# Thirty-two experts, 96 places each, packed four to three tiles of 128 rows

## The chip, the cores and the metric

The kernel runs on one core of one Trainium2 chip. The metric is the device time of one execution in microseconds (us), lower is better. All arithmetic is in float32. The core has a matrix engine (PE, with its weight loads shown as PEld), three engines for elementwise work (DVE, ACT, POOL), a queue engine that mostly issues transfers (SP), and 16 DMA engines.

## The reference, cut to what matters

One layer of a decoder over 1024 prompt tokens and 8 sample tokens. Projections, sparse attention, a gated spatial mixer and the first layer norm come first and are not touched by the change. What matters is the last part, a mixture of experts: 4 groups of 8 experts, each token takes the best group and the best two experts in it.

```python
def hierarchical_moe(x, ...):
    lg = (xt @ w_router_group + b_router_group)
    gsel = jnp.argmax(lg, axis=-1)
    ...
    vals, eidx = lax.top_k(le_sel, 2)
    pw = jax.nn.softmax(vals, axis=-1) * pgsel[:, None]
    ...
    for g in range(N_GROUPS):          # 4 groups of 8 experts
        hg = silu(einsum('td,edf->tef', xt, w_expert_gate[g])) * einsum('td,edf->tef', xt, w_expert_up[g])
        out = out + einsum('tef,efd->td', hg * wg[:, :, None], w_expert_down[g])
```

Here d is 1024 and f is 256, so an expert has 2 MB of gate and up weights and 1 MB of down weights. 1032 tokens with two experts each give 2064 (token, expert) pairs, 64.5 for an expert on average. Counted from the reference's inputs, the fullest expert has 82 and none has over 96.

## The kernel before, in words

The program is a row of stages, each its own block of five engine programs joined by a barrier. Two of them matter here.

`merge_and_route` (L1353 to L1677) goes through 9 tiles of 128 tokens. PE multiplies by `w_o` (`project`, L1515), DVE adds and normalizes, PE turns the rows and makes the router's logits (`route`), DVE picks the two experts (`pick`, L1607), PE counts how many earlier tokens chose each expert (`rank`, L1545), and DVE makes of rank and expert the address of the pair in a table in device memory, `list_of` (`place`, L1627). POOL writes the two entries of each token with indirect DMAs (L1487). Before, expert e with rank r has the address 32 r + e, so that column e of a 128 x 32 table holds the first 128 pairs of expert e. SP loads the weights of experts 0 and 1 in this stage (L1461, L1462; `W_AHEAD` is 2).

`experts` (L1680 to L1908) then runs once for ranks 0 to 127. A second pass (L2178) is run only if an expert has more than 128 pairs. For each expert, POOL gathers 128 rows of `h` with an indirect DMA (L1760), whatever the number of real entries; PE turns them in 8 transposes (`turn_rows`, L1796); PE makes gate and up, 128 x 512, over 8 slices of the contraction (`make_hidden`, L1786); ACT and DVE make silu(gate) * up; PE turns that (`turn_hidden`, L1804) and makes the result, 128 x 1024, over 2 slices (`make_result`, L1813); ACT and DVE copy it out; POOL scatters it to `pair_out` (L1768), leaving out the rows of empty entries. The weights stand in `W_BUFS` = 4 buffers. A single semaphore per buffer, `w_in`, stands for both its transfers. Each float32 matmul of the program is two passes, that is two MATMUL and two LDWEIGHTS instructions in the trace.

What sets the order is `staggered`, a written software pipeline: at step i PE runs `turn_hidden(i-2)`, `make_hidden(i-1)`, `turn_rows(i)`, `make_result(i-2)`. A hardware loop covers four experts in its body. POOL goes in program order: gather e, then scatter e - 3, each after its waits. SP goes in program order too: the table's entries, then experts 2 and 3 (behind `rows_in`, so that the first two gathers come first), then expert e as soon as both halves of the result of expert e - 4 are made (L1744, semaphore `down`). `Finish` is the last stage's work: it loads `pair_out`, adds the two halves with PE (L1984, L1994) and makes the second layer norm.

Of the kernel before, what the change touches and what calls it, by code (L numbers as in the profile page):

```python
# [13 lines left out]
I32 = mybir.dt.int32  # L14
U32 = mybir.dt.uint32
ALU = mybir.AluOpType
# [3 lines left out]
P = 128  # L20
D = 1024
# [1325 lines left out]
W_AHEAD = 2  # L1347
SLOTS = TOK * N_EXPERTS
# [4 lines left out]
def merge_and_route(nc, ins, outs, keep, scratch):  # L1353

    with nc.cleanup_on_exit(), ExitStack() as ctx:
# [26 lines left out]
        fall, expert = sb("fall", [P, N_EXPERTS]), sb("expert", [P, N_EXPERTS])  # L1382
# [7 lines left out]
        choice = [[sb(f"choice{n}_{j}", [P, N_EXPERTS]) for j in range(2)] for n in range(2)]  # L1390
        both = [sb(f"both{j}", [P, N_EXPERTS]) for j in range(2)]
# [31 lines left out]
        N_CONST = 10  # L1423
# [4 lines left out]
        def _(sp):  # L1428
# [7 lines left out]
            def load_constants():  # L1436
                for to, name in ((ln1[:, 0, :], "ln1_g"), (ln1[:, 1, :], "ln1_b"), (b_r[:], "b_router"),
                                 (minus_half[:], "minus_half"), (fall[:], "fall"), (expert[:], "expert"),
# [20 lines left out]

            for j in range(W_AHEAD):  # L1460
                sp.dma_start(keep["w_gate_up"][j][:], ins["w_gate_up"][j]).then_inc(keep["w_in"][j], 16)  # L1461
                sp.dma_start(keep["w_down"][j][:], ins["w_down"][j]).then_inc(keep["w_in"][j], 16)  # L1462
# [32 lines left out]
        def _(pe):  # L1495
# [49 lines left out]
            def rank(i):  # L1545
# [3 lines left out]
                nc.tensor.matmul(to, earlier[:], both[i % 2][:], start=True, stop=False)  # L1549
# [33 lines left out]
        def _(dve):  # L1583
# [23 lines left out]
            def pick(i):  # L1607
# [11 lines left out]
                    one[:], marked, highest[:], None, ALU.is_equal)))  # L1619
                step(V.scalar_tensor_tensor(rest, one[:], -3.0e30, rest, ALU.mult, ALU.add))  # L1620
                first_of(rest, best2[:, col], N_EXPERTS, lambda: step(V.tensor_scalar(
                    two[:], marked, highest[:], None, ALU.is_equal)))
                step(V.tensor_tensor(both[i % 2][:], one[:], two[:], ALU.add))
                step(V.tensor_scalar(both[i % 2][:], both[i % 2][:], valid[:, col], None, ALU.mult))
                V.tensor_tensor(chosen[:, i + 1, :], chosen[:, i, :], both[i % 2][:], ALU.add).then_inc(picked, 1)

            def place(i):  # L1627
# [52 lines left out]
def experts(nc, ins, outs, keep, scratch, chunk, loaded, tag):  # L1680


    with nc.cleanup_on_exit(), ExitStack() as ctx:  # L1683
# [39 lines left out]
        def _(sp):  # L1723
# [537 lines left out]
```

## Time and profile before

| what | us |
|---|---|
| median of 3 runs | 1551.05 (1545.45 to 1553.15) |
| the profiled execution | 1560.32 |
| its span | 1558.7 |
| PE busy in it | 1439.7 (92%) |
| DVE busy | 724.5 (46%) |
| ACT busy | 297.2 (19%) |
| mean DMA rate over the span | 142 GB/s |

The profiled execution is 9.3 us above the median of the timed runs, so differences are worked out in it and then taken from the median. PE is busy nearly everywhere, but a kernel of stages has to be read stage by stage: the expert stage, from 1125.8 us to 1503.8 us, is the one that the change rebuilds.

### The profile page before, as it was taken

The numbers are of one execution on the slowest core, as the hardware profiler recorded it, in microseconds if no ns is written. First come the engines' busy times: TensorE is split into PE (matmuls) and PEld (weight loads), VectorE is DVE, ScalarE is ACT, GpSimd is POOL, SyncE is SP. The second block draws the span as 40 slices with busy tenths as digits, with TensorE's granted clock in tenths as the row PEclk, the third lists the DMA queues.
The fourth block names the chain that finished last, engine by engine and source line by source line (L and its number), as shares of the span: only waits on it lengthen the run. The fifth ranks groups of instructions, "written<-read, shape, count | busy, mean of one in ns | idle before, by whom it ended". The sixth has DMA issues, their size and how long they took to land. (4 is left out here: it accounts for less than half of the span.)

```text
span 1558.7 us, 17701 instructions
## 1 busy us (share of the span) xinstructions
PE 1439.7 (92%) x5707; PEld 782.1 (50%) x5707; DVE 724.5 (46%) x1639; ACT 297.2 (19%) x656; POOL 254.4 (16%) x308
## 2 busy tenths in 40 slices
PE   7999999799999999898989898999489999999985
PEld 2444444344566666565757564555244444444431
DVE  0201023788888889954648444566411111111125
ACT  0100122221221111102554200000011111111114
POOL 3131000133310000201351000011112111121103
PEclk9999999799999999998999899999689999999998
DMA  9221001400122111101331196111089999989835
GB/s 312 69 65 35 15 15 69 129 0 1 41 95 75 70 61 61 70 19 51 92 92 62 55 345 260 28 37 32 15 334 337 347 342 345 352 337 354 325 125 227
DMA packets 72474, 221.89 MB, mean 142 GB/s; under 512 B 16634, under 2 KB 42234, under 8 KB 62042
## 3 DMA queue, kind: packets, MB, share of 16 engines
q1 hardware_dynamic: 56138, 184.64, 33.0%
q0 software_dynamic: 14992, 35.90, 6.6%
q8 instruction: 38, 0.62, 0.2%
q10 hardware_dynamic: 1280, 0.53, 0.2%
q14 instruction: 26, 0.21, 0.0%
HBM read 190.56 MB, written 38.84 MB: 147 GB/s over the span
## 5 line engine op out<-in xcount | busy, mean ns | idle before, releaser
L1786 PE MATMUL main_ps_experts<-w_gate_up,main_e_rowsT 128*128 128x512 f32 x512 | 227.7, 598 | 1.2 <-DVE main_e_rowsT L1891 1.2
L906 DVE TENSOR_SCALAR_CACHE_REDUCE front<-score,bound 128x384 bf16<-128x384 f32 (+2 forms) x198 | 174.2, 943 | 19.2 <-DVE bound L932 18.9
L234 PE MATMUL ps_front<-front,x_all 128*128 128x512 f32 (+1 forms) x448 | 180.4, 557 | 1.7 <-ACT wi L364 1.7
L1786 PEld LDWEIGHTS main_ps_experts<-w_gate_up,main_e_rowsT 128*128 128x128 f32 x512 | 95.7, 192 | 110.6 <-issue 110.6
L234 PEld LDWEIGHTS ps_front<-front,x_all 128*128 128x128 f32 x448 | 83.2, 190 | 91.7 <-issue 81.2
L1896 DVE TENSOR_TENSOR main_hidden<-main_hidden,main_ps_experts 128x256 f32<-128x256 f32 x32 | 13.5, 421 | 221.1 <-ACT main_hidden L1843 221.1
L1520 PE MATMUL ps_merge<-w_o,mergedT 128*128 128x512 f32 x256 | 113.4, 601 | 3.0 <-DVE h_rows L1651 3.0
L733 PE MATMUL ps_gate<-x_all,w_gate 128*128 128x344 f32 x384 | 116.0, 461 | 0.0
L1813 PE MATMUL main_ps_experts<-w_down,main_hiddenT 128*128 128x512 f32 x256 | 115.3, 593 | 0.5 <-ACT main_hiddenT L1848 0.5
L733 PE MATMUL ps_gate<-x_all,front 128*128 128x344 f32 x384 | 113.2, 453 | 0.0
L733 PEld LDWEIGHTS ps_gate<-x_all,w_gate 128*128 128x128 f32 x384 | 74.3, 194 | 38.9 <-issue 2.4
L733 PEld LDWEIGHTS ps_gate<-x_all,front 128*128 128x128 f32 x384 | 72.7, 190 | 37.5
L1520 PEld LDWEIGHTS ps_merge<-w_o,mergedT 128*128 128x128 f32 x256 | 48.5, 192 | 62.5 <-issue 58.2
L1768 POOL DMA_INDIRECT pair_out<-main_result,entries x32 | 31.8, 993 | 291.8 <-DVE main_result L1903 291.8
L906 DVE TENSOR_SCALAR_CACHE_REDUCE front<-score_s,bound 8x2049 bf16<-8x2049 f32 x33 | 77.0, 2334 | 0.0
L1813 PEld LDWEIGHTS main_ps_experts<-w_down,main_hiddenT 128*128 128x128 f32 x256 | 46.2, 190 | 47.1 <-issue 46.4
L888 POOL TENSOR_TENSOR front<-front 128x344 f32<-128x344 f32 x24 | 26.8, 1116 | 255.9 <-ACT front L848 255.9
L1903 DVE COPY main_result<-main_ps_experts 128x512 f32<-128x512 f32 x32 | 22.1, 692 | 89.9 <-PE main_ps_experts L1813 89.9
L681 PE MATMUL ps_gate<-early,x_all 128*128 128x512 f32 x128 | 58.3, 598 | 4.4 <-ACT u L790 4.4
L845 ACT ACTIVATE front<-ps_gate,gate_bias 128x344 f32<-128x344 f32 x48 | 26.1, 547 | 185.9 <-PE ps_gate L733 185.9
L1501 PE MATMUL ps_merge<-attnT,w_a 128*128 128x344 f32 x192 | 58.6, 470 | 3.3 <-PEq L985 3.3
L681 PE MATMUL ps_gate<-front,x_all 128*128 128x512 f32 x128 | 57.5, 592 | 0.0
(296 smaller groups left out, 1784.0 us busy)
## 6 DMA issues: line engine op xcount, KB each, us to landing
w_gate_up<-in_w_gate_up SPq DMA_DIRECT2D x32, 2048.0 KB, 8.7
w_down<-in_w_down SPq DMA_DIRECT2D x32, 1024.0 KB, 11.9
w_gate_up<-pair_out SPq DMA_DIRECT2D x8, 1024.0 KB, 12.0
front<-in_w_qkvi SPq DMA_DIRECT2D x8, 930.0 KB, 20.0
w_gate<-in_w_gate SPq DMA_DIRECT2D x4, 1280.0 KB, 6.0
front<-in_w_gate SPq DMA_DIRECT2D x4, 1280.0 KB, 5.9
h_rows<-in_x_rows SPq DMA_DIRECT2D x9, 512.0 KB, 6.0
h<-h_rows SPq DMA_DIRECT2D x18, 256.0 KB
```

Source lines behind the costliest of these rows:

```text
L234: mm = nc.tensor.matmul(ps[:, g % 2, 0:c1 - c0], x_all[:, k, t * P:(t + 1) * P], w[:, k, c0:c1], start=(k == 0), stop=(k == KC - 1))
L681: mm = nc.tensor.matmul(ps[:, b, :], x_all[:, k, t * P:(t + 1) * P], w_uv(k)[:, b * GW:(b + 1) * GW], start=(k == 0), stop=(k == KC - 1))
L733: mm = nc.tensor.matmul(ps[:, SETS[at % 2][which], 0:n], w_gate[j][:, which * KC + k, :], right[:, k, c0:c0 + n], start=(k == 0), stop=(k ...
L845: op = nc.scalar.activation(to, src, ACT.Sigmoid, bias=gate_bias[:, which, bass.ds(i * 2 + j, 1)])
L888: nc.gpsimd.tensor_tensor(m[:, 1, 0:n], m[:, 1, 0:n], m[:, 2, 0:n], ALU.mult).then_inc(multiplied, 1)
L906: V.tensor_scalar(waste[0:n, at - width:at], s, column(bound, g), None, compare, ALU.add, accum_out=column(number, g)).then_inc(taken, 1)
L1501: mm = nc.tensor.matmul(ps[:, 3 + n % 3, 0:width], w_a[:, k, blk * P:(blk + 1) * P], attnT[:, k, c0:c0 + width], start=(k == 0), stop=(k = ...
L1520: mm = nc.tensor.matmul(ps[:, c, :], mergedT[:, k, t * P:(t + 1) * P], w_o[:, k, c * 512:(c + 1) * 512], start=(k == 0), stop=(k == KC - 1))
L1768: pool.indirect_dma_start(out=scratch["pair_out"].rearrange("t w q j d -> (t w q j) d"), out_offset=bass.IndirectOffsetOnAxis(ap=entries[: ...
L1786: mm = nc.tensor.matmul(ps[:, GU, :], rowsT[j][:, k, :], w_gu[jw][:, k, :], start=(k == 0), stop=(k == KC - 1))
L1813: mm = nc.tensor.matmul(ps[:, 4 + 2 * j + c, :], hiddenT[j][:, k, :], w_dn[jw][:, k, c * 512:(c + 1) * 512], start=(k == 0), stop=(k == F ...
L1903: nc.vector.tensor_copy(result[j][:, 512:D], ps[:, 5 + 2 * j, :]).then_inc(down_dve, 1)
```

## The change

Four experts now share three tiles (packs) of 128 rows, 32 x 4 = 128 places of the 384 for ranks of 0 to 95 each. So there are 24 packs where there were 32 expert tiles, and the second pass is run if an expert has over 96 pairs. Pack 0 of a quad holds 96 rows of its expert 0 and 32 of expert 1; pack 1 holds 64 rows of expert 1 and 64 of expert 2; pack 2 holds 32 rows of expert 2 and 96 of expert 3.

```diff
+SHARE = 96
+QUAD = 4
+PACKS = N_EXPERTS // QUAD * 3
+PARTS = (((0, 32, 0), (32, 64, 0), (64, 96, 0), (96, 128, 1)), ((0, 64, 1), (64, 128, 2)),
+         ((0, 32, 2), (32, 64, 3), (64, 96, 3), (96, 128, 3)))
...
                 for k in range(KC):
-                    mm = nc.tensor.matmul(ps[:, GU, :], rowsT[j][:, k, :], w_gu[jw][:, k, :], start=(k == 0), stop=(k == KC - 1))
+                    for c0, c1, b in PARTS[s % 3]:
+                        mm = nc.tensor.matmul(ps[c0:c1, GU, :], rowsT[j][:, k, c0:c1], w_gu[b][:, k, :],
+                                              start=(k == 0), stop=(k == KC - 1))
...
-            for j in range(loaded, W_BUFS):
-                if j >= 2:
-                    sp.wait_ge(rows_in[j - 2], 16)
-                load(j, j)
+            for e in range(loaded, W_BUFS):
+                load_gate_up(e)
+                load_down(e)
...
-            with sp.Fori(1, N_EXPERTS // W_BUFS) as i:
-                for j in range(W_BUFS):
-                    sp.wait_ge(down, (i * W_BUFS + (j - W_BUFS)) * 2 + 2)
-                    load(i * W_BUFS + j, j)
+            for g in range(1, N_EXPERTS // QUAD):
+                e, s = g * QUAD, 3 * (g - 1)
+                sp.wait_ge(gate_up, s + 1)
+                load_gate_up(e)
+                sp.wait_ge(gate_up, s + 2)
+                load_gate_up(e + 1)
+                sp.wait_ge(down, 2 * s + 2)
+                load_down(e)
+                sp.wait_ge(gate_up, s + 3)
+                load_gate_up(e + 2)
+                load_gate_up(e + 3)
+                sp.wait_ge(down, 2 * s + 4)
+                load_down(e + 1)
+                sp.wait_ge(down, 2 * s + 6)
+                load_down(e + 2)
+                load_down(e + 3)
...
-                step(V.scalar_tensor_tensor(marked, ps[:, 3 + i % 2, 0:N_EXPERTS], float(N_EXPERTS), expert[:],
-                                            ALU.mult, ALU.add))
+                ranks = ps[:, 3 + i % 2, 0:N_EXPERTS]
+                step(V.tensor_scalar(share, ranks, 683.0, None, ALU.mult))
+                step(V.tensor_scalar(share, share, 16, None, ALU.logical_shift_right))
+                step(V.scalar_tensor_tensor(lin, share, -float(SHARE), ranks, ALU.mult, ALU.add), wait=False)
+                step(V.scalar_tensor_tensor(address, share, float(P * PACKS), column[:], ALU.mult, ALU.add))
+                step(V.tensor_tensor(lin, lin, lane[:], ALU.add))
+                step(V.tensor_scalar(wrap, lin, float(P), None, ALU.is_ge))
+                step(V.scalar_tensor_tensor(wrap, lin, float(2 * P), wrap, ALU.is_ge, ALU.add), wait=False)
+                step(V.scalar_tensor_tensor(address, lin, float(PACKS), address, ALU.mult, ALU.add))
+                step(V.scalar_tensor_tensor(marked, wrap, 1.0 - P * PACKS, address, ALU.mult, ALU.add))
                 for which in range(2):
-                    step(V.tensor_tensor(waste, choice[which][i % 2][:], marked, ALU.mult))
-                    step(V.tensor_reduce(slot[:, which:which + 1], waste, AX.X, ALU.add))
+                    step(V.scalar_tensor_tensor(waste, choice[which][i % 2], 1.0, marked, ALU.mult, ALU.mult,
+                                                accum_out=slot[:, which:which + 1]))
...
-        with nc.If(longest > P):
-            with nc.Fori(1, (longest + (P - 1)) // P) as chunk:
+        with nc.If(longest > SHARE):
+            with nc.Fori(1, (longest + (SHARE - 1)) // SHARE) as chunk:
```

`make_result` has its four or two column groups in the same way. `w_in` is split into `w_gu_in` for gate and up and `w_dn_in` for down, and PE waits for the first at `make_hidden` and the second at `make_result`. The hardware loops of PE, ACT, DVE and SP in this stage become straight code (`loop=False`). Some small tiles of `merge_and_route` move into room left free in `attnT`, and one more small constant is loaded.

PE in the middle of the expert stage: one step of the pipeline before, with `ident` the identity of the transposes.

```order
L1804 MATMUL main_ps_experts<-ident,main_hidden 128x128 x2
L1782 REGISTER_ALU
L1786 MATMUL main_ps_experts<-w_gate_up,main_e_rowsT 128x512 x8
L1796 MATMUL main_ps_experts<-ident,main_e_rows 128x128 x8
L1813 MATMUL main_ps_experts<-w_down,main_hiddenT 128x512 x4
```

The same stage of the changed kernel, two steps in a row.

```order
L1838 MATMUL main_ps_experts<-ident,main_hidden 128x128 x2
L1819 MATMUL main_ps_experts<-w_gate_up,main_e_rowsT 32x512 x32
L1830 MATMUL main_ps_experts<-ident,main_e_rows 128x128 x8
L1849 MATMUL main_ps_experts<-w_down,main_hiddenT 64x512 x8
L1838 MATMUL main_ps_experts<-ident,main_hidden 128x128 x2
L1819 MATMUL main_ps_experts<-w_gate_up,main_e_rowsT 32x512 x32
L1830 MATMUL main_ps_experts<-ident,main_e_rows 128x128 x8
L1849 MATMUL main_ps_experts<-w_down,main_hiddenT 32x512 x16
```

The order of the four pieces of a step stays; a piece of 8 full matmuls has become one of 32 matmuls of 32 columns, or of 16 of 64 columns, and every step goes from full width to column groups and back twice.

DVE in `place`, before, for one of the nine tiles of tokens.

```order
L1631 SCALAR_TENSOR_TENSOR attnT<-ps_merge,expert 128x32
L1634 TENSOR_TENSOR attnT<-choice_0,attnT 128x32
L1635 TENSOR_REDUCE slot<-attnT 128x1
L1634 TENSOR_TENSOR attnT<-choice_0,attnT 128x32
L1635 TENSOR_REDUCE slot<-attnT 128x1
L1636 TENSOR_TENSOR slot_out<-slot,away 128x2
```

The same in the changed kernel.

```order
L1640 TENSOR_SCALAR attnT<-ps_merge 128x32
L1641 TENSOR_SCALAR attnT<-attnT 128x32
L1642 SCALAR_TENSOR_TENSOR attnT<-attnT,ps_merge 128x32
L1643 SCALAR_TENSOR_TENSOR attnT<-attnT,column 128x32
L1644 TENSOR_TENSOR attnT<-attnT,lane 128x32
L1645 TENSOR_SCALAR attnT<-attnT 128x32
L1646 SCALAR_TENSOR_TENSOR attnT<-attnT 128x32
L1647 SCALAR_TENSOR_TENSOR attnT<-attnT 128x32
L1648 SCALAR_TENSOR_TENSOR attnT<-attnT 128x32
L1650 SCALAR_TENSOR_TENSOR attnT,slot<-attnT 128x32 x2
L1652 TENSOR_TENSOR slot_out<-slot,away 128x2
```

Six instructions have become twelve, at the same place between the norm of one tile and the pick of another.

## Rows read from the trace of the kernel before

**Rows 1.** The page: chain that ended last, shares of the span.

```profile
PE main_ps_experts L1786 14%; PE main_ps_experts L1813 7%; PE main_ps_experts L1796 2%; PE main_ps_experts L1994 1%; PE main_ps_experts L1984 1%; PE main_ps_experts L1804 0%; DMA w_gate_up<-pair_out 0%; DMA main_e_rows<-h,tokens 0%; DMA pair_out<-main_result,entries 0%; DVE h_rows L2050 0%; DMA entries<-list_of 0%; DVE main_e_rowsT L1891 0%; ACT h_rows L2008 0%; DVE main_result L1903 0%; DVEq L1683 0%
```

**Rows 2.** Chain in order of time, one step: start us, us, what.

```profile
1158.61 6.87 PE main_ps_experts L1786 x16
1165.47 0.87 PE main_ps_experts L1796 x8
1166.35 3.44 PE main_ps_experts L1813 x8
1169.78 0.22 PE main_ps_experts L1804 x2
```

**Rows 3.** Windows: length, busy us of five engines, PE clock, DMA share, GB/s.

```profile
1136.00:1150.00 14.00, 13.60 (x33) 6.03 (x33) 1.11 (x2) 1.34 (x3) 0.93 (x1) 0.83 0.99 414
1161.40:1480.60 319.20, 319.20 (x954) 155.68 (x953) 50.51 (x84) 53.91 (x112) 54.74 (x56) 1.00 0.91 344
```

**Rows 4.** DMA issues: count, KB each, median us from issue to landing.

```profile
w_gate_up<-in_w_gate_up SPq DMA_DIRECT2D x32, 2048.0 KB, 8.7
w_down<-in_w_down SPq DMA_DIRECT2D x32, 1024.0 KB, 11.9
...
main_e_rows<-h,tokens POOLq DMA_INDIRECT x32, 10.2
pair_out<-main_result,entries POOLq DMA_INDIRECT x32, 9.4
```

**Rows 5.** Timeline of SP in that stage, two experts' loads.

```profile
1215.55 0.33 SPq L1725 DMA_DIRECT2D w_gate_up<-in_w_gate_up  x1
1216.07 0.40 SPq L1726 DMA_DIRECT2D w_down<-in_w_down  x1
1226.94 0.33 SPq L1725 DMA_DIRECT2D w_gate_up<-in_w_gate_up  x1
```

**Rows 6.** Timeline, matmuls of 32 columns in four groups, in the merge stage.

```profile
946.94 3.64 PE L1510 MATMUL ps_merge<-w_o,mergedT 128*32 128x512 f32 x32 [2.47 <-DVE mergedT L1597]
```

**Rows 7.** Timeline of `Finish`: full width and 64 columns in turn.

```profile
1520.53 1.94 PE L1994 MATMUL main_ps_experts<-w_gate_up,attnT 128*64 128x512 f32 x8
1522.40 1.98 PE L1984 MATMUL main_ps_experts<-h_rows,main_f_grown 128*128 128x512 f32 x4
1524.31 1.94 PE L1994 MATMUL main_ps_experts<-w_gate_up,attnT 128*64 128x512 f32 x8
```

**Rows 8.** Chain in order of time, the expert stage's start.

```profile
1128.53 4.06 DMA main_e_rows<-h,tokens
...
1132.63 1.98 PE main_ps_experts L1796 x8
...
1135.58 9.68 PE main_ps_experts L1786 x16
```

**Rows 9.** Timeline of DVE and POOL, merge stage, a tile and the tail.

```profile
1096.35 1.28 DVE L1657 SCALAR_TENSOR_TENSOR h_rows<-h_rows,ps_merge 128x512 f32<-128x512 f32 x2 [5.31 <-PE ps_merge L1520]
...
1111.07 0.20 DVE L1666 TENSOR_TENSOR router_logits<-ps_merge,b_r 128x36 f32<-128x36 f32 x1 [1.81 <-PE ps_merge L1543]
1111.18 0.18 DVE L1631 SCALAR_TENSOR_TENSOR attnT<-ps_merge,expert 128x32 f32<-128x32 f32 x1
...
1117.63 0.19 DVE L1631 SCALAR_TENSOR_TENSOR attnT<-ps_merge,expert 128x32 f32<-128x32 f32 x1 [1.16 <-PE ps_merge L1550]
1117.86 0.19 DVE L1634 TENSOR_TENSOR attnT<-choice,attnT 128x32 f32<-128x32 f32 x1
...
1118.75 0.16 DVE L1636 TENSOR_TENSOR slot_out<-slot,away 128x2 uint32<-128x2 f32 x1
1119.70 0.97 POOL L1487 DMA_INDIRECT list_of<-entry,slot_out  x1 [4.21 <-DVE slot_out L1636]
```

**Rows 10.** Timeline of DVE in `Finish`, the read of an accumulator.

```profile
1514.73 0.07 DVE L2061 DVE_READ_ACCUMULATOR h_rows<-h_rows,attnT 8x1 f32 x1
```

**Rows 11.** Timeline of PE, end of the expert stage and what follows.

```profile
1500.09 3.70 PE L1813 MATMUL main_ps_experts<-w_down,main_hiddenT 128*128 128x512 f32 x8 [0.46 <-ACT main_hiddenT L1848]
...
1514.01 3.68 PE L1994 MATMUL main_ps_experts<-w_gate_up,attnT 128*64 128x512 f32 x8 [4.90 <-DMA w_gate_up<-pair_out]
```

More of the change, by code:

```diff
@@ L1380, in merge_and_route @@
         empty = h[:, TILES - 1, 0:SLOTS // P].bitcast(U32)
-        fall, expert = sb("fall", [P, N_EXPERTS]), sb("expert", [P, N_EXPERTS])
+        fall, lane, column = (sb(n, [P, N_EXPERTS]) for n in ("fall", "lane", "column"))
         valid, away = sb("valid", [P, TILES]), sb("away", [P, TILES])
@@ L1389, in merge_and_route @@
         lgT = over[0:ROUTER, D + 3 * N_EXPERTS:D + 3 * N_EXPERTS + P]
-        choice = [[sb(f"choice{n}_{j}", [P, N_EXPERTS]) for j in range(2)] for n in range(2)]
-        both = [sb(f"both{j}", [P, N_EXPERTS]) for j in range(2)]
+        FREE = D + 3 * N_EXPERTS + P
+        free = [over[:, FREE + n * N_EXPERTS:FREE + (n + 1) * N_EXPERTS] for n in range(10)]
+        choice = [free[2 * n:2 * n + 2] for n in range(2)]
+        both = free[4:6]
+        share, lin, address, wrap = free[6].bitcast(I32), free[7], free[8], free[9]
         slot = sb("slot", [P, 2])
@@ L1618, in pick @@
                 first_of(rest, best1[:, col], N_EXPERTS, lambda: step(V.tensor_scalar(
-                    one[:], marked, highest[:], None, ALU.is_equal)))
-                step(V.scalar_tensor_tensor(rest, one[:], -3.0e30, rest, ALU.mult, ALU.add))
+                    one, marked, highest[:], None, ALU.is_equal)))
+                step(V.scalar_tensor_tensor(rest, one, -3.0e30, rest, ALU.mult, ALU.add))
                 first_of(rest, best2[:, col], N_EXPERTS, lambda: step(V.tensor_scalar(
[L1622 to L1625, printed above, removed]
+                    two, marked, highest[:], None, ALU.is_equal)))
+                step(V.tensor_tensor(both[i % 2], one, two, ALU.add))
+                step(V.tensor_scalar(both[i % 2], both[i % 2], valid[:, col], None, ALU.mult))
+                V.tensor_tensor(chosen[:, i + 1, :], chosen[:, i, :], both[i % 2], ALU.add).then_inc(picked, 1)
             def place(i):
@@ L1688, in sem @@
             return nc.alloc_semaphore(f"{tag}_{name}")
-        ident, tokens, entries, w_gu, w_dn = (keep[n] for n in ("ident", "tokens", "entries", "w_gate_up", "w_down"))
-        w_in = keep["w_in"] if loaded else [sem(f"w_in{j}") for j in range(W_BUFS)]
+        ident, w_gu, w_dn = (keep[n] for n in ("ident", "w_gate_up", "w_down"))
+        tokens, entries = (keep[n][:, 0:PACKS] for n in ("tokens", "entries"))
+        w_gu_in, w_dn_in = (keep[n] if loaded else [sem(f"{n}{j}") for j in range(W_BUFS)] for n in ("w_gu_in", "w_dn_in"))
         rows = [sb(f"e_rows{j}", [P, D]) for j in range(2)]
@@ L1754, in _ @@
             pool.wait_ge(tokens_ready, 1)
-            for e in range(N_EXPERTS + 3):
-                if e < N_EXPERTS:
+            for e in range(PACKS + 3):
+                if e < PACKS:
                     if e >= 2:
@@ L2162, in build @@
         keep["w_down"] = [sb(f"w_down{j}", [P, F // P, D], side="right") for j in range(W_AHEAD)]
-        keep["w_in"] = [whole.enter_context(nc.semaphore(f"w_in_expert{j}")) for j in range(W_BUFS)]
+        keep["w_gu_in"], keep["w_dn_in"] = ([whole.enter_context(nc.semaphore(f"{n}_expert{j}")) for j in range(W_BUFS)]
+                                            for n in ("w_gu_in", "w_dn_in"))
         for name, shape, dt in (("router_logits", [P, TILES, ROUTER], F32), ("weights", [P, 2, TILES], F32),
```

63 lines of the change are left out of this document (35 added, 28 removed).

## The prediction

> **What bounds the kernel now.** I read the chain that ended last first: the expert stage's matmuls hold it, L1786 and L1813 ahead of all else [rows 1]. Then the chain in order of time: one step of that stage is 6.87 + 0.87 + 3.44 + 0.22 = 11.4 us of PE work with nothing between the pieces [rows 2], and the loads of the next expert start 11.39 us apart [rows 5]. The window over 28 such steps has PE busy for all of its 319.2 us at clock 1.00 [rows 3]. So PE sets the pace, 31 steps after the first.
>
> The same window tells what is next. The DMA engines are busy 0.91 of it and move 344 GB/s [rows 3], that is 3.92 MB in 11.4 us: 3.15 MB of weights (2048 + 1024 KB, [rows 4]), 0.52 MB for the gather of 128 rows of 4 KB, and 0.25 MB left for the scatter. The weights don't become fewer by packing. Whoever takes PE steps away has to ask how fast DMA can go.
>
> **What the change removes.** 32 steps become 24, so after the first there are 23 in place of 31. At the old pace that would be 8 x 11.4 = 91 us. Two things make the steps longer.
>
> **PE's step.** A tile of mixed rows is computed in column groups, each with other weights streaming. The question is if groups run beside each other. The merge stage has the same form: 32 passes of 512 columns in groups of 32 took 3.64 us [rows 6], while 8 passes at full width take 3.44 us in the chain [rows 2]. Four groups thus cost what one full pass costs. The groups of 64 in the last stage say the same: 8 passes start 1.87 us ahead of the next piece, against 4 x 0.43 = 1.72 us for as much at full width [rows 7]. What is left is the change of width: 1.87 - 1.72 = 0.15 us one way and (1524.31 - 1522.40) - 1.72 = 0.19 us the other way [rows 7]. A step changes width four times (the two pieces of transposes stay full width), which is 0.7 us, so PE's step is 12.1 us. The bounds are 11.4 (the change of width is hidden behind the short transposes) and 12.6 (0.3 a time, since four groups may drain worse than two).
>
> The Trainium skill ("TensorE: Matmul & The Clock Gate", Measured speedup vs the span model) gives a packing of four tiles 3.07 times one tile's speed and of three 2.38 times. The trace of this case has 4 x 3.44 / 3.64 = 3.8 times for long accumulations [rows 2, 6]; what the rule would make of the time is a rival below.
>
> **DMA's step.** A pack needs 4/3 of an expert's weights, 4.19 MB, a gather of 0.52 MB, and 0.25 x 32/24 = 0.34 MB of scatter: 5.05 MB. In the 14 us at the stage's start in which loads stood in the queue all the time, the rate was 414 GB/s at a share of 0.99 [rows 3]. The long window, taken to a share of one, gives 344 / 0.91 = 378, but it has a gap and a slow restart in each step, since the next load waits for `down`. In the changed kernel gate and up are loaded as soon as `gate_up` frees a buffer, some transfer is nearly always queued, so the 414 row is the nearer one; for more gathers and scatters beside the weights I take 405. That gives 5.05 / 0.405 = 12.5 us, with 12.2 (414) and 13.4 (378) as bounds. PE's 12.1 and DMA's 12.5 are almost level; the greater holds: **12.5 us a step**. The first five steps find their weights loaded or on the way and go at 12.1.
>
> 23 steps are then 18 x 12.5 + 5 x 12.1 = 285.5 us where there were 31 x 11.4 = 353.4: **-67.9 us**.
>
> **The start of the stage.** SP no longer waits for `rows_in` before it loads experts 2 and 3, so the first gather goes out beside 6.3 MB of weights. Alone it took 4.06 us [rows 8]; beside weights it takes 10.2 us in the median [rows 4]. Nothing on PE can start before it, and PE's queue holds the whole pipeline behind that wait. **+6.1 us**, with 0 (it overtakes the loads, whose first bytes come later) and +9 (it stands behind the whole of the queue: 6.3 MB at 414 GB/s from 1126 on end at 1141, against 1132.6) as bounds; I take the middle one because it is the measured value in just this company. The first `make_hidden`, 9.68 us against 6.87 at full clock [rows 2, 8], stays as slow.
>
> **Placing.** `place` took 1117.63 to 1118.91, 1.28 us for six instructions 0.22 us apart [rows 9]. Now it has nine short ones of 0.22 or so, two with an accumulator (0.22 + 0.07 and a little for the step between, 0.32, [rows 9, 10]) and the last of 0.16: 2.8 us, so +1.5 us a tile. In the tiles' loop DVE waits 5.31 us for PE [rows 9], which covers it. Two of the nine stand where nothing covers: `place` at 1111.18, behind which `pick`, `rank` and the last `place` follow one on another, and the last at 1117.63, for which POOL waits to write the table [rows 9]. The one before them delays the last `rank` by a little. **+3.3 us** (3.0 to 3.8).
>
> **What costs nothing.** ACT and DVE do 24 times what they did 32 times, both under 60 us in 319 [rows 3]. The scatters move as many rows. POOL's gather is issued a step ahead of its use, and 10.2 us of landing fit in a step of 12. SP's straight code waits in turn for `gate_up` and `down`: behind each wait stand the loads that follow, and the worst is the next quad's first gate load, held back until the last result of the quad before; it is needed almost two steps later, and its 2 MB take 5 us. That cover is gone only where the rate is under 380. The end stays: the last result, then 10 us to the loads of `pair_out` and `Finish` [rows 11].
>
> **Sum.** -67.9 + 6.1 + 3.3 = -58.5 us. In the profiled execution, 1560.3 becomes 1501.8; it lay 9.3 above the median of the runs, and the forecast is for the median: 1551 - 58.5 = **1492 us**.
>
> **Rivals.**
> *DMA is slower than the start shows.* For it speaks that the long window has 378 at full share, and that four buffers can't hide every wait of SP. With 13.4 us a step: 18 x 0.9 = 16 us more, 1508; with still 5% less (14.1 us), 1520. The Trainium skill ("DMA: Bandwidth & Descriptors", Specifications) names about 358 GB/s as the limit of device memory for one core. By that rule the step would be 14.1 us as well; the window at 414 GB/s contradicts it for as long as 14 us.
> *Groups overlap less than in the short row.* If long runs reach only 3.1 of 4 (2.4 of 3), the column pieces of 10.3 us become 13.3, the step 15.1, and two groups perhaps 13: mean 14.4. 23 x 14.4 = 331, -22 + 9.4 = -13 us: 1538. Against it stands that [rows 6] was taken with four streams from four addresses and with loads in flight.
> *Slower than before.* Three of four groups in packs 0 and 2 stream the same slice of weights at the same time, which no row shows. If same addresses made them go one after the other, such a pack would need 3 x 10.3 + 1.8 = 32.7 us, pack 1 12.1, mean 25.8: 23 x 25.8 - 353 + 9 = +250 us, 1800. It decides from a mean step of (353.4 - 9.4) / 23 = 15.0 us up: above that, the change loses.
> *It isn't 24 packs.* If an expert had over 96 pairs, the second pass would run and cost another stage, near 300 us. The count from the inputs is 82 at most.
> *Better than forecast.* Width changes hidden, DMA at 420 GB/s, the first gather not delayed: 12.0 a step gives 23 x 12.0 = 276, -77 + 3 = -74: 1477.
>
> **Chances.** Forecast, a step of 12.1 to 13.2 us (1480 to 1505): 0.60. Better (1465 to 1480): 0.12. Slow DMA (1505 to 1530): 0.16. Poor overlap (1530 to 1555): 0.07. Slower (same-address groups, 0.04; a second pass, 0.01): 0.05. A measurement of this kernel can tell about 0.5% from no change, 8 us. Faster by more than that: 0.60 + 0.12 + 0.16 + 0.05 = 0.93; within it 0.02; slower 0.05. The range 1470 to 1522 leaves out a little of the better case, a third of slow DMA and all below it: 0.8.
>
> **What would show it.** Right: in the expert stage PE pieces of 32 groups' passes as long as the full-width ones (6.9 to 7.2 us), a step near 12.5, DMA share near 1 with over 400 GB/s, short waits of PE for `w_gate_up`, the first gather's landing near 10 us, and `entries` loaded 3 us later than before. Wrong: pieces of over 8 us (overlap), a rate under 385 with share 1 and PE waiting for weights in every quad (DMA), gaps in the DMA rate while PE waits (SP's order of waits), or PE waiting on its own sequencer now that the loops are gone.

## The result, and the profile after

The changed kernel takes 1477.62 us in the median of its executions, the kernel before 1550.23 us beside it: a ratio of 0.954 (0.951 to 0.958), 72.6 us less. The forecast was 1492 us. Direction and mechanism came as forecast, the size is 14 us beyond it, inside the range.

One execution of the changed kernel took 6210 us (and one of `all_three_beside` below 7917 us), with matmuls some five times as long also in stages that the change doesn't touch: such executions are left out. All rows of "after" come from another profiled execution of the same kernel (labelled `after_again` below, span 1497.3 us).

The chain that ended last, shares of the span by engine and line, after:

```profile
PE main_ps_experts L1819 12%; PE main_ps_experts L1849 6%; PE main_ps_experts L1830 2%; PE main_ps_experts L2030 1%; PE main_ps_experts L2020 1%; DMA main_e_rows<-h,tokens 1%; PE main_ps_experts L1838 1%; DMA w_gate_up<-pair_out 0%; DVE h_rows L2086 0%; DMA pair_out<-main_result,entries 0%; DMA entries<-list_of 0%; DVE main_e_rowsT L1927 0%; ACT h_rows L2044 0%; DVE main_result L1939 0%; DVEq L1699 0%
```

It is the same chain as in [rows 1] with the lines shifted: PE's two large pieces still lead it, with smaller shares of a shorter span. No line of weights appears in it. The chain in order of time (start us, us, what), one step, which answers to [rows 2]:

```profile
1257.57 7.00 PE main_ps_experts L1819 x64
1264.57 1.02 PE main_ps_experts L1830 x8
1265.59 3.57 PE main_ps_experts L1849 x32
1269.16 0.37 PE main_ps_experts L1838 x2
```

Every piece is 0.13 to 0.15 us longer than at full width: 11.96 us against 11.40. So four groups of 32 columns, here with three of them on the same slice of weights, run beside each other without any other loss. Windows (length, busy us of five engines, PE clock, DMA share, GB/s), against [rows 3]:

```profile
1200.00:1400.00 200.00, 199.43 (x1496) 69.07 (x1494) 29.98 (x50) 31.85 (x67) 32.25 (x33) 1.00 1.01 419
```

Both are full: PE is busy for 199.4 of 200 us, and the DMA engines move 419 GB/s at a share of one. In [rows 3] it was 344 GB/s at 0.91. PE's waits in the pieces of the stage, 1120 to 1460 us (who waits <- for what: sum us, times, largest us):

```profile
PE main_ps_experts L1830 <- DMA main_e_rows<-h,tokens: 11.6, 1, 11.6
PE main_ps_experts L1819 <- issue: 2.8, 2, 2.3
PE main_ps_experts L1819 <- DVE main_e_rowsT L1927: 1.6, 2, 1.0
```

The first gather is the one long wait. "Issue" means that the profile shows nobody that was waited for. I take these waits for waits on a buffer of weights, since they are gone in `half_loads` below, where only the loads were cut. Behind the longer of the two, `make_hidden` took 8.73 us instead of 7.07, and the granted clock lay near the lower of its two levels (1.2 GHz, shown as 0.50) in the first part of it. The piece in PE's timeline, and a window:

```profile
1404.25 8.73 PE L1819 MATMUL main_ps_experts<-w_gate_up,main_e_rowsT 128*32 128x512 f32 x64 [2.26 <-issue]
```

```profile
1404.25:1408.00 3.75, 3.75 (x20) 1.04 (x24) 0.00 (x0) 0.00 (x0) 0.96 (x1) 0.55 0.98 414
```

That one piece cost 1.7 us more. `gather_first` below had a wait of 2.25 us at the same place and its piece took 7.07; `two_changes` had one of 2.22 us and 8.77. So it doesn't come behind every such wait. The start of the stage in the chain, against [rows 8], with that gather:

```profile
1137.74 9.49 DMA main_e_rows<-h,tokens
1147.27 1.98 PE main_ps_experts L1830 x8
```

It landed in 9.49 us where it had taken 4.06.

The stages before the experts, which most of these runs leave alone, end up to 26 us earlier or later from one execution to another, so the stages are measured between marks: the matmul that counts the chosen pairs (`main_ps_experts<-chosen,ones`, right after the merge stage), and the end of the last `make_result`. A mean step, here and below, is taken between starts of `turn_hidden` without the first and the last interval, where the pipeline fills and empties; in the table it is counted for all 31 or 23 steps.

| us | before | after | difference |
|---|---|---|---|
| last `rank` in the merge loop to the mark (placing, the table of places) | 26.06 | 28.69 | +2.6 |
| mark to the last result's end (the expert stage) | 377.95 | 309.92 | -68.0 |
| of it, mark to the first gather's rows in use | 6.79 | 12.20 | +5.4 |
| of it, mean step | 11.397 (31) | 12.20 (23) | -72.7 |
| last result to the span's end | 54.91 | 52.31 | -2.6 |
| sum | | | -68.0 |

The runs of that launch have 1494.67 against 1563.61 us, -68.9 us, so the marks hold all of it. What is left of the stage, -0.7 us, lies in its first and last steps. The end's 2.6 us weren't forecast. They lie in pieces that didn't change. In the chain, the start of `Finish` after, and then the second of its two lines before:

```profile
1454.58 2.88 PE main_ps_experts L2030 x8
1457.46 2.62 PE main_ps_experts L2020 x4
```

```profile
1517.69 2.91 PE main_ps_experts L1984 x4
```

The first eight matmuls took 3.68 us before [rows 11]. Their granted clock is 0.65 instead of 0.50. These two pieces are 1.1 us of the 2.6. Another 0.6 us is the landing of the last scatter and of the first load of `pair_out` (2.69 and 4.83 us instead of 3.18 and 4.99), and 0.9 us the landing of the last results at the very end (8.05 us from the end of their issue to the end of the span instead of 8.9). No experiment was made on any of them. The same end takes 51.8 to 53.1 us in the other runs of the changed kernel and 53.9 us in `before_groups`.

### The profile page after: what moved, and what is told of

Its sections match the earlier page's. It is cut to its first block and busy times, and to the rows that moved or that the text cites. A ratio compares the mean times of both kernels' runs of the same rounds, so it can differ in the third digit from the quotient of the medians.

```text
span 6209.0 us, 19396 instructions
## 1 busy us (share of the span) xinstructions
PE 6114.6 (98%) x6779; PEld 2250.8 (36%) x6779; DVE 712.0 (11%) x1687; ACT 284.0 (5%) x624; POOL 234.4 (4%) x292
## 5 line engine op out<-in xcount | busy, mean ns | idle before, releaser
L234 PE MATMUL ps_front<-front,x_all 128*128 128x512 f32 (+1 forms) x448 | 1087.9, 2768 | 1.7 <-ACT wi L364 1.7
L1819 PE MATMUL main_ps_experts<-w_gate_up,main_e_rowsT 128*32 128x512 f32 (+1 forms) x1280 | 632.1, 1911 | 1.1 <-DVE main_e_rowsT L1927 1.0
L234 PEld LDWEIGHTS ps_front<-front,x_all 128*128 128x128 f32 x448 | 389.0, 889 | 663.9 <-issue 663.8
L733 PE MATMUL ps_gate<-x_all,w_gate 128*128 128x344 f32 x384 | 613.5, 1944 | 0.0
L733 PE MATMUL ps_gate<-x_all,front 128*128 128x344 f32 x384 | 556.4, 1776 | 0.0
L1528 PE MATMUL ps_merge<-w_o,mergedT 128*128 128x512 f32 x256 | 422.2, 1926 | 3.0 <-DVE h_rows L1667 3.0
L733 PEld LDWEIGHTS ps_gate<-x_all,w_gate 128*128 128x128 f32 x384 | 303.1, 791 | 301.9 <-issue 301.8
L681 PE MATMUL ps_gate<-early,x_all 128*128 128x512 f32 x128 | 345.6, 3024 | 4.4 <-ACT u L790 4.4
L681 PE MATMUL ps_gate<-front,x_all 128*128 128x512 f32 x128 | 344.1, 3027 | 0.0
L1849 PE MATMUL main_ps_experts<-w_down,main_hiddenT 128*32 128x512 f32 (+1 forms) x640 | 317.0, 1898 | 0.5 <-ACT main_hiddenT L1884 0.5
L219 PE MATMUL ps_front<-front,x_all 128*128 128x512 f32 (+1 forms) x64 | 158.0, 2790 | 0.0
## 6 DMA issues: line engine op xcount, KB each, us to landing
w_gate_up<-in_w_gate_up SPq DMA_DIRECT2D x32, 2048.0 KB, 12.5
```

The lines of the kernel that those rows point to most:

```text
L219: mm = nc.tensor.matmul(ps[:, FIRST_BANKS[b], 0:c1 - c0], x_all[:, k, 0:P], w[:, k, c0:c1], start=(k == 0), stop=(k == KC - 1))
L234: mm = nc.tensor.matmul(ps[:, g % 2, 0:c1 - c0], x_all[:, k, t * P:(t + 1) * P], w[:, k, c0:c1], start=(k == 0), stop=(k == KC - 1))
L681: mm = nc.tensor.matmul(ps[:, b, :], x_all[:, k, t * P:(t + 1) * P], w_uv(k)[:, b * GW:(b + 1) * GW], start=(k == 0), stop=(k == KC - 1))
L733: mm = nc.tensor.matmul(ps[:, SETS[at % 2][which], 0:n], w_gate[j][:, which * KC + k, :], right[:, k, c0:c0 + n], start=(k == 0), stop=(k ...
L1528: mm = nc.tensor.matmul(ps[:, c, :], mergedT[:, k, t * P:(t + 1) * P], w_o[:, k, c * 512:(c + 1) * 512], start=(k == 0), stop=(k == KC - 1))
L1819: mm = nc.tensor.matmul(ps[c0:c1, GU, :], rowsT[j][:, k, c0:c1], w_gu[b][:, k, :], start=(k == 0), stop=(k == KC - 1))
```

## Experiments

The ratio is always to the kernel before on the same chip in the same launch. "Stage" is mark to last result, as in the table. The stage of one and the same kernel differs between executions, too: 309.9 us in `after_again`, 306.6 us in `after_beside`. So stages of different runs that are under 3 us apart show nothing by themselves. Two limits are to be told apart: PE (12.0 a step, groups and their changes of width) and DMA (12.0 to 12.1 a step, 5.05 MB at 420 GB/s).

**The changed kernel again** (`after_again`, no edit). It gives the rows above.

> The changed kernel once more, for a profile in an undisturbed execution. The time should be 1478 us as in the five runs, ratio 0.954. Theory A (PE sets the pace again, DMA keeps up): the steps of the expert stage are 12.1 us apart, PE hardly waits for w_gate_up or w_down after the first steps, the DMA rate is over 414 GB/s. Theory B (DMA sets the pace): steps of over 12.3 us, PE waits for weights in each quad, DMA share near 1.

Measured: 1494.67 against 1563.61, 0.9552 (0.9517 to 0.9587). The mean of the steps is 12.20, and those without a wait take 11.98. The price of DMA in the forecast (12.5 a step) is too high.

**Full width in place of groups** (`full_width`). All places of a pack take one expert's weights, so the mixed packs compute something else; the loads stay.

```diff
-PARTS = (((0, 32, 0), (32, 64, 0), (64, 96, 0), (96, 128, 1)), ((0, 64, 1), (64, 128, 2)),
-         ((0, 32, 2), (32, 64, 3), (64, 96, 3), (96, 128, 3)))
+PARTS = (((0, 128, 0),), ((0, 128, 1),), ((0, 128, 3),))
```

> Each pack is computed at full width with the weights of one expert only (rows of the pack's other experts get the wrong weights); loads, gathers, scatters and the 24 packs stay. It takes away the column groups and the changes of width. Theory A (PE sets the pace at 12.1 us): a step falls to 11.4 if DMA could follow, but 5.05 MB in 11.4 us would be 443 GB/s, so DMA takes over at about 12.0: 0 to 8 us less than the changed kernel. Theory B (DMA sets the pace now): no difference, within 3 us. If groups overlapped badly: over 30 us less.

Measured: 1490.91 against 1563.61, 0.9538 (0.9505 to 0.9570); stage 302.20, mean step 11.90. Its waits of PE and its window:

```profile
PE main_ps_experts L1818 <- issue: 8.6, 6, 2.1
```

```profile
1200.00:1400.00 200.00, 192.47 (x572) 93.16 (x570) 30.17 (x51) 32.38 (x67) 32.25 (x33) 1.00 1.01 421
```

PE's pieces are back at 11.4, but only 0.3 of the 0.57 us come out: PE now stands six times for weights, and DMA runs at 421 GB/s with a share of one. The mean of 11.90 isn't DMA's own step yet, since the first steps found their weights loaded and went at 11.4. From then on every third `make_hidden` starts when its weights land. Two of those starts in PE's timeline:

```profile
1256.53 7.11 PE L1818 MATMUL main_ps_experts<-w_gate_up,main_e_rowsT 128*128 128x512 f32 x16 [1.82 <-issue]
1401.38 7.11 PE L1818 MATMUL main_ps_experts<-w_gate_up,main_e_rowsT 128*128 128x512 f32 x16 [1.40 <-issue]
```

They are 12 steps and 144.85 us apart. So DMA's own step is 12.07 us, 0.1 above PE's own (11.975, `half_loads` below). The expectations of some runs below were written with 11.9 for it.

**Groups in the kernel before** (`before_groups`). Nothing is packed; every matmul of `make_hidden` and `make_result` is done in four groups of 32 columns.

```diff
-mm = nc.tensor.matmul(ps[:, GU, :], rowsT[j][:, k, :], w_gu[jw][:, k, :], start=(k == 0), stop=(k == KC - 1))
+for c0 in range(0, P, 32):
+    mm = nc.tensor.matmul(ps[c0:c0 + 32, GU, :], rowsT[j][:, k, c0:c0 + 32], w_gu[jw][:, k, :],
+                          start=(k == 0), stop=(k == KC - 1))
```

> The kernel before, with 32 expert tiles of one expert each, but every matmul of the experts as four column groups of 32 that stream the same slice of the same weights. It prices column groups alone, where DMA has room. My sum (four changes of width a step, 0.7 us): 32 x 0.7 = 22 us slower than before, 1573 us; the step 12.1. If the changes hide behind the short transposes: no change, 1551. If groups that read the same address went one after the other: over 900 us slower.

Measured: 1580.15 against 1563.61, 1.0124 (1.0090 to 1.0157); stage 394.5, 16.55 us longer, mean step 11.968. One step of its chain, and a window:

```profile
1190.38 7.00 PE main_ps_experts L1787 x64
1197.39 1.02 PE main_ps_experts L1798 x8
1198.41 3.57 PE main_ps_experts L1816 x32
1201.98 0.37 PE main_ps_experts L1806 x2
```

```profile
1160.00:1460.00 300.00, 300.00 (x2662) 99.61 (x2658) 45.13 (x75) 48.25 (x100) 49.01 (x50) 1.00 0.86 329
```

The pieces are those of the changed kernel to the hundredth, with all four groups streaming the same weights, and with DMA at 329 GB/s. The price of the groups is 0.57 us a step, paid at the four changes of width (0.14 each), and neither the address nor the load on DMA has a part in it. 31 x 0.57 = 17.7 us against the 16.55 measured; the first `make_hidden` happened to be 1.2 us shorter than before (8.48 against 9.68).

**The first gather ahead of the loads** (`gather_first`). The wait that the change had taken out is put back for the loads of experts 2 and 3.

```diff
 for e in range(loaded, W_BUFS):
+    if e >= 2:
+        sp.wait_ge(rows_in[e - 2], 16)
     load_gate_up(e)
```

> The changed kernel with the wait for the first two gathers put back before the loads of experts 2 and 3. My sum: the first gather lands after 4 us in place of 10, so the stage starts 6.1 us earlier; weights come up to 7 us later but have slack at the start: 6 us less than the changed kernel, 1472 us. Rival: DMA sets the pace, so bytes delayed at the start are paid back later: 0 to 3 us less, or more time.

Measured: 1487.17 against 1563.61, 0.9510 (0.9476 to 0.9544); stage 303.38, 6.5 us less than after; mark to rows in use 6.98. Its chain and window:

```profile
1137.56 4.34 DMA main_e_rows<-h,tokens
1141.94 1.98 PE main_ps_experts L1832 x8
```

```profile
1200.00:1400.00 200.00, 196.10 (x1482) 68.00 (x1478) 29.90 (x50) 31.84 (x66) 32.80 (x34) 1.00 1.01 420
```

The gather takes 4.34 us again, and PE starts 5.2 us earlier after the mark. The delayed loads cost little: PE later waits 3.9 us for weights instead of 2.8, as DMA at 420 GB/s has no reserve from which to catch up. The rest of the 6.5 us is in two pieces behind waits: the first `make_hidden` took 8.66 us instead of 9.45, and the one of 8.73 us doesn't occur. The intervals of the two ratios overlap, so the whole time doesn't show the gain; the gather's row in the chain does.

**Half of the loads** (`half_loads`). From expert 4 on only half of each buffer is loaded; matmuls take what stands in the rest, so the results are not those of the reference.

```diff
-sp.dma_start(w_gu[e % W_BUFS][:], ins["w_gate_up"][e]).then_inc(w_gu_in[e % W_BUFS], 16)
+n = KC if e < QUAD else KC // 2
+sp.dma_start(w_gu[e % W_BUFS][:, 0:n, :], ins["w_gate_up"][e][:, 0:n, :]).then_inc(w_gu_in[e % W_BUFS], 16)
...
```

`w_down` is halved in the same way.

> The changed kernel, but from the second quad on only half of each expert's weights is loaded (the other half of each buffer keeps the first quad's values, so the experts' outputs are wrong). DMA's step falls from 11.9 to about 7 us; PE's stays at 11.98. What I have now (both limits level, PE a hair above): only the waits for weights go, 4 to 7 us less than the changed kernel. If DMA contention also slowed PE's own pieces: more than 10 us less, pieces shorter than 7.00 us. If DMA were the one bound: 30 us or more less.

Measured: 1487.02 against 1562.33, 0.9535 (0.9499 to 0.9571); stage 304.97, mean step 11.975.

```profile
1200.00:1400.00 200.00, 200.00 (x1518) 67.77 (x1510) 29.55 (x49) 31.25 (x66) 33.25 (x34) 1.00 0.72 252
```

PE is busy for all of the window at 252 GB/s, and its pieces are unchanged (7.00, 3.57). This is PE's own step: 11.975 us. Weights cost the changed kernel 5 us in all in `after_again` (309.92 - 304.97), 1.7 of them in the one piece at a low clock, and 1.6 us in `after_beside` (306.58).

**Loads behind whole packs** (`late_loads`). Each expert's gate and up of the next quad are loaded together with its down weights, behind the last result made from that buffer, in place of behind the last `make_hidden` that reads it. The next quad's first pair waits for one pack's result, the second for two, the last two for three.

```diff
-sp.wait_ge(gate_up, s + 1)
-load_gate_up(e)
-sp.wait_ge(gate_up, s + 2)
-load_gate_up(e + 1)
 sp.wait_ge(down, 2 * s + 2)
+load_gate_up(e)
 load_down(e)
-sp.wait_ge(gate_up, s + 3)
-load_gate_up(e + 2)
-load_gate_up(e + 3)
 sp.wait_ge(down, 2 * s + 4)
+load_gate_up(e + 1)
 load_down(e + 1)
 sp.wait_ge(down, 2 * s + 6)
+load_gate_up(e + 2)
 load_down(e + 2)
+load_gate_up(e + 3)
 load_down(e + 3)
```

> The changed kernel with every load held back until the results that used its buffer are made (the rule of the kernel before: gate and up and down of an expert go together, behind down). It undoes the early loads alone. Since DMA at 420 GB/s needs 11.9 of every 12.0 us, any hole that the late rule leaves is paid in full: in a quad of 36 us the queue is empty for 3 to 6 us, so 8 quads cost 20 to 45 us, and PE waits for w_gate_up at the first pack of each quad. Rival: buffers four deep suffice for the late rule too, under 5 us.

Measured: 1646.95 against 1562.33, 1.0540 (1.0508 to 1.0573): slower than the kernel before; stage 461.0, 151 us longer than after, mean of all 23 steps 18.7. My expectation (20 to 45 us) was far too low. Its waits, its chain around one of them and a window:

```profile
PE main_ps_experts L1816 <- issue: 62.5, 7, 9.5
PE main_ps_experts L1816 <- DMA w_gate_up<-in_w_gate_up: 61.7, 7, 9.2
```

```profile
1184.76 9.46 issue
1194.22 9.11 PE main_ps_experts L1816 x64
...
1207.98 8.69 DMA w_gate_up<-in_w_gate_up
...
1216.72 9.82 PE main_ps_experts L1816 x32
...
1231.50 7.00 PE main_ps_experts L1816 x64
```

```profile
1200.00:1560.00 360.00, 250.97 (x1694) 82.84 (x1686) 34.29 (x57) 36.66 (x76) 36.22 (x37) 0.83 0.67 257
```

Twice in each quad, 14 times in all, PE stands some 9 us for a load of 2 MB that could only be issued when the step before it ended: 124 us. Behind such a wait `make_hidden` takes 8.8 to 9.8 us in PE's timeline instead of 7.1: 31 us more in all 14. The two sums make up the 151 us and the 4.5 us that the changed kernel loses in the same way. The start of one of them in a window:

```profile
1194.22:1198.20 3.98, 3.98 (x20) 1.09 (x24) 0.00 (x0) 0.00 (x0) 0.00 (x0) 0.50 0.55 225
```

The granted clock is at its lower level there, and 0.83 in the mean of the long window. The step that does no waiting has 7.00 in the chain again. DMA is idle a third of the time in this kernel. Where four buffers hold three steps of work, each load must go out as soon as the last matmul that reads its buffer is done.

**No gather for empty places** (`skip_empty`, on `gather_first`). An empty place gathers the row of the last token; now it is left out, but for the first two packs.

```diff
-V.tensor_scalar(tokens, tokens, float(TOK - 1), None, ALU.min).then_inc(tokens_ready, 1)
+V.tensor_scalar(tokens[:, 0:2], tokens[:, 0:2], float(TOK - 1), None, ALU.min).then_inc(tokens_ready, 1)
...
-in_offset=bass.IndirectOffsetOnAxis(ap=tokens[:, e:e + 1], axis=0)
+in_offset=bass.IndirectOffsetOnAxis(ap=tokens[:, e:e + 1], axis=0),
+bounds_check=TOK - 1, oob_is_err=False
```

> The kernel with the first gather ahead of the loads (gather_first), and gathers that leave out the empty places: 2064 rows and the padding of the first two packs in place of 3072, 4 MB fewer of about 120. DMA's step falls from 11.9 to about 11.5 us. If DMA's small excess at each quad is what PE waits for: the waits of PE for weights go, 4 to 5 us less than gather_first, ratio 0.948. If PE alone sets the pace: no difference from gather_first, 0.951.

Measured: 1486.61 against 1562.33, 0.9512 (0.9482 to 0.9542); stage 300.01, 3.4 us less than `gather_first`; mean step 11.99.

```profile
1200.00:1400.00 200.00, 199.88 (x1508) 68.38 (x1508) 30.66 (x51) 32.74 (x68) 32.54 (x33) 1.00 1.00 411
```

With fewer bytes (411 GB/s at a step of 11.99 is 4.93 MB) PE has hardly a gap left, and the step is PE's own. The gain in the stage is what DMA had been late in `gather_first`; the ratios of the two runs (0.9512 and 0.9510) show no difference.

**Fewer changes of width** (`two_changes`, on `gather_first`). The two pieces of transposes stand together, then the two in column groups. For that `turn_rows` goes to the head of the step, ahead of `turn_hidden`; ACT and DVE read in the same order, and the scatters come a step later.

```diff
-staggered(pe, PACKS, [(2, turn_hidden), (1, make_hidden), (0, turn_rows), (2, make_result)], 2, loop=False)
+staggered(pe, PACKS, [(0, turn_rows), (2, turn_hidden), (1, make_hidden), (2, make_result)], 2, loop=False)
```

> gather_first with turn_rows put ahead of turn_hidden and make_hidden, so that the two pieces of transposes are neighbours and a step changes width twice in place of four times; each scatter goes one place later in POOL's order so that the gather has time. PE's step falls from 11.98 to 11.7. With DMA at 11.9 that should give little: 0 to 3 us less than gather_first, with longer waits of PE for weights. If PE alone set the pace: 23 x 0.28 = 6 us less.

Measured: 1483.46 against 1562.33, 0.9496 (0.9467 to 0.9525); stage 304.19, mean step 12.173: no gain on `gather_first` (303.38) that could be told from the 3 us between two executions. Its waits of PE and a window:

```profile
PE main_ps_experts L1821 <- issue: 3.7, 3, 2.2
PE main_ps_experts L1851 <- DMA w_down<-in_w_down: 2.5, 4, 1.3
```

```profile
1200.00:1400.00 200.00, 194.65 (x1482) 72.60 (x1478) 30.25 (x50) 31.84 (x66) 32.34 (x33) 0.99 1.01 421
```

PE's pieces did become shorter, but it now waits 6.2 us for weights, at 421 GB/s, and one `make_hidden` behind such a wait took 8.77 us. A saving of 0.2 to 0.3 us on PE's step brings nothing here that shows, as long as DMA has no more to give.

**Both on top of the first gather** (`all_three`).

> gather_first, two_changes and skip_empty together: PE's step 11.7 us, DMA's about 11.5 (skip_empty alone had DMA free of PE's waits, two_changes alone had PE waiting for weights 6 us in all). If two levels stand beside each other, lowering both gives what neither gave: 23 x 0.28 = 6 us less than gather_first, ratio 0.947, and no waits of PE for weights. Rival: the DMA queue can't give up more because its share is 1.00 even with fewer bytes: as two_changes, 0.950.

Measured: 1468.32 against 1545.77, 0.9494 (0.9469 to 0.9519); stage 296.23, mean step 11.773. Two steps of its chain, and a window:

```profile
1240.88 7.02 PE main_ps_experts L1821 x32
1247.90 3.57 PE main_ps_experts L1851 x32
1251.47 1.02 PE main_ps_experts L1832 x8
1252.49 0.22 PE main_ps_experts L1840 x2
1252.71 7.00 PE main_ps_experts L1821 x64
1259.72 3.58 PE main_ps_experts L1851 x16
...
1271.55 3.43 PE main_ps_experts L1851 x32
```

```profile
1200.00:1400.00 200.00, 199.28 (x1528) 70.13 (x1522) 29.99 (x50) 32.23 (x67) 31.27 (x31) 1.00 0.96 394
```

With DMA relieved, the shorter pieces come out: 0.2 us a step less than `skip_empty`, 3.8 us over the stage. In another execution (`all_three_beside` below) the stage took 298.38 us, with 2.4 us of waits for weights instead of 0.7, so this gain is 1.6 to 3.8 us. The chain shows why not more. The second transpose piece is back at 0.22, but the two pieces in groups are not always alike: 32 columns against the 64 of the middle pack (x32 behind x32, x16 behind x64) cost a change of their own, 3.57 and 3.58, and only 32 behind 32 gives 3.43. So there are two changes in one step of three and three in the others, 2.67 in the mean. 11.40 + 2.67 x 0.14 = 11.77, what was measured.

**Full width and half of the loads** (`full_half`). Both edits together; neither limit is left.

> full_width and half_loads together (wrong weights for part of the rows, and half of each later expert's weights not loaded). full_width alone gave 4 us, half_loads alone about 4 to 7. With both limits lifted PE's step should be 11.4: against the changed kernel 23 x 0.58 = 13 us and its waits for weights, 4 us: 17 us less, ratio 0.944 to 0.945. If the two small gains only add: 10 us less, 0.949.

Measured: 1463.44 against 1545.77, 0.9470 (0.9442 to 0.9498); stage 292.17, mean step 11.397, the step of the kernel before to the thousandth.

```profile
1200.00:1400.00 200.00, 199.54 (x594) 97.15 (x592) 31.79 (x53) 34.07 (x71) 31.31 (x32) 1.00 0.66 235
```

The four corners stand together now (mean step, us):

| | all loads | half of the loads |
|---|---|---|
| column groups | 12.20 (12.05 in `after_beside`) | 11.975 |
| full width | 11.90 | 11.397 |

Taking DMA away alone gives 0.23 (0.08), taking the groups away alone gives 0.30 (0.15), both give 0.80 (0.65); in brackets from the 12.05 of the second execution. The four cells come from three launches. Two limits at almost one height: each hides most of the other's saving.

**The changed kernel and the best version side by side** (`after_beside`, `all_three_beside`, no further edits).

> The changed kernel again, on the same chip and in the same rounds as the best version, since executions differ by 5 to 10 us in the stages before the experts from chip to chip. Expert stage 310 us, 69 to 73 us less than before in all, ratio 0.954 to 0.955.

> The best version beside it. The traces put its expert stage at 296.2 us against 309.9 of the changed kernel, so 13.7 us less than after_beside: ratio about 0.946. If the gain of the two lowered levels is given back elsewhere (its first comparison, 0.9494, was no better than two_changes with 0.9496): 5 to 8 us less, 0.950.

Measured: 1477.70 against 1469.26, with 1550.14 for the kernel before: 0.9543 (0.9516 to 0.9569) and 0.9473 (0.9449 to 0.9497). The intervals are apart, and the stage is 8.2 us shorter (306.58 to 298.38), the whole 8.4. I had expected 13.7, from stages taken on two chips: the changed kernel's own step here was 12.05 instead of 12.20, since it waited only 1.6 us for weights, and the stage of the best version was 2.2 us longer than in `all_three`. How long PE waits for weights thus differs from execution to execution, where DMA has no reserve. The version with all three edits is the fastest here that leaves no part of the work out.

## Why the prediction was right, and where it was off

**What bounds the kernel.** Right: PE set the pace before, and DMA was next. The steps are 24 as counted.

**PE's step.** Forecast 12.1, measured 11.975. Both parts of it hold. The groups run side by side in long accumulations (7.00 us for what full width does in 6.87), and what they cost is the change of width, 0.14 us each instead of the 0.17 read from [rows 7]. The groups of three on one slice of weights, which no row showed, cost nothing. The Trainium skill ("TensorE: Matmul & The Clock Gate", Measured speedup vs the span model) gives 3.07 times one tile's speed for four row tiles, and 2.38 times for three column tiles. The four column groups of this case have 4 x 6.87 / 7.00 = 3.93, if one group alone is counted as a pass at full width.

**DMA's step.** This term failed. "for more gathers and scatters beside the weights I take 405" was a discount on the 414 of [rows 3] for which no row stood, and 414 itself was not the top. Measured are 419 to 421 GB/s at a share of 1.01 over 200 us, in the changed kernel and in three of the experiments. The step of DMA is 12.07 us (`full_width`), where the forecast had 12.5, and 5.05 MB at 421 would be 12.0. The other end of the range, the long window taken to a share of one (378), was no measure of the rate at all: in that kernel DMA was not what was waited for. The Trainium skill ("DMA: Bandwidth & Descriptors", Specifications) names some 358 GB/s as device memory's limit for one core, which is half of what two cores share. This kernel runs on one core, and its windows are 17% above that.

With PE at 11.98 and DMA at 12.07, taking the larger of the two ("the greater holds") is right within 0.13: 12.20 and 12.05 were measured in two executions, and 0.08 of the 12.20 is the one piece at a low clock. So DMA is above PE as the forecast had it, but by 0.1 and not by 0.4 us. With the measured step the term is 23 x 12.20 - 353.3 = -72.7 instead of -67.9, 4.8 us of the difference.

**The first gather.** Right in mechanism and size: +6.1 forecast, +5.4 measured, and `gather_first` gives 5.2 of it back. The gather landed in 9.5 us beside 6.3 MB of weights; in [rows 4] it was 10.2 among weights.

**Placing.** Forecast +3.3, measured +2.6: +1.1 instead of +1.5 for a call of `place` that nothing covers. The nine short instructions cost less than 0.22 each; the first and last of the last call in DVE's timeline after, against [rows 9], are

```profile
1125.76 0.19 DVE L1640 TENSOR_SCALAR attnT<-ps_merge 128x32 int32<-128x32 f32 x1 [1.16 <-PE ps_merge L1558]
...
1127.98 0.16 DVE L1652 TENSOR_TENSOR slot_out<-slot,away 128x2 uint32<-128x2 f32 x1
```

that is 2.38 us for the call where it was 1.28.

**What was to cost nothing.** SP's order of waits did, as forecast, and `late_loads` shows how much hung on it: 151 us if gate and up wait for a pack's result. The end was to stay; it became 2.6 us shorter, 1.1 of it by the clock, for which the forecast had no term.

**The sum.** By the marks the terms are -72.7 for the steps, -0.7 in the first and last, +5.4, +2.6, -2.6: -68.0, against -58.5 forecast. Of the 9.5 us, 4.8 are the step with DMA's rate in it, 0.7 each the gather, the placing and the stage's ends, and 2.6 the end. The remaining 4 to 5 us to the 72.6 of the medians are no more than what two launches of the same pair of kernels differ by (68.9 and 72.6). That 1477.6 lies outside the band of 1480 to 1505 us, to which the forecast gave 0.60, is thus in part chance: 1551 - 68.0 = 1483 would lie inside.

**The rivals.** "Better than forecast" is what happened: 1477 (1465 to 1480), with 12.0 a step and DMA at 420 GB/s, though its reasons are only in part right: the rate is, but the changes of width are not hidden, the first gather is delayed, and the steps are 12.05 to 12.2. It had 0.12 against the 0.60 of the forecast, and the 14 us stretch at 414 GB/s should have given it more. Slow DMA is excluded by the rate, poor overlap and same addresses by `before_groups`, a second pass by the 24 steps.

## What to carry to other kernels

When a change removes work from the engine that sets the pace, compute the next limit's step too, and if the two lie within a few per cent, expect a later saving on one of them alone to bring only part of its size (PE's pieces 0.57 us shorter gave 0.30, half of the loads 0.23, both together 0.80; from a second execution of the changed kernel 0.15, 0.08 and 0.65). Take a DMA rate from a stretch in which transfers really queued, at share one and without a discount, and never scale up one from a stretch in which they waited. With few buffers, release each as soon as its last reader is done: the same loads in a coarser order lost twice what the whole change had won.

## What the runs showed of the hardware

- Matmuls of 32 columns in four column groups, three or all four of them with the same weights streaming, take 7.00 us for 16 full passes' work that takes 6.87 us at full width. The price is 0.13 to 0.15 us at each change of width, also from 32 to 64 columns, and it stands in the piece behind the change.
- One core's 16 DMA engines moved 419 to 421 GB/s over 200 us, beside gathers and scatters. When PE's pieces became shorter (`full_width`) the rate stayed at 421 GB/s and PE waited for weights, so the rate was a limit there.
- A gather of 128 rows of 4 KB landed in 4.1 to 4.3 us with no loads ahead of it, and in 9.5 us beside the loads of two experts.
- After waits of 9 us PE's `make_hidden` ran in 8.8 to 9.8 us instead of 7.1. The granted clock was 0.50 in the first 4 us of one of them, and 0.83 over the stage that had 14 such waits; in `after_again` it was 1.00 over 200 us. One wait of 2.26 us was followed by a piece of 8.73 us at 0.55, another of 2.25 us in another run was not.
